# Copy and square before the exponentials: the order of ScalarE's steps in a gated recurrence over heads

## What is computed

```python
def hgrn2_mixer(h, lb, w_in, o_norm, w_o):      # 8 heads, DK = DV = 128, chunks of C = 32
    q_x, f_x, i_x, g_x = jnp.split(h @ w_in, ...)
    f = lb + (1.0 - lb) * sigmoid(f_x)
    q = heads(silu(q_x));  k = heads(1.0 - f);  log_f = heads(log(f));  v = heads(i_x)
    b = cumsum(log_f, axis=3)                    # within a chunk
    q_rel = q * exp(b - b_ref);  k_rel = k * exp(b_ref - b)
    a = where(causal, q_rel @ k_rel.T, 0.0)
    o_intra = a @ v
    q_dec = q * exp(b);  k_dec = k * exp(b_last - b);  chunk_decay = exp(b_last)
    def step(state, xs):                         # over the 16 chunks
        o_inter = qd @ state
        state = dec[..., None] * state + kd.T @ vc
        return state, o_inter
    o = o_intra + o_inter
    o = rms_norm(o, o_norm) * silu(g_x)
    return o @ w_o
```

## Time and profile before

| what | value |
|---|---|
| median of 3 runs | 1892.64 us (1892.26 to 1893.92) |
| the profiled execution | 1893.63 us, its span 1891.7 us |
| TensorE busy over the span | 1697.2 us (90%) |
| VectorE, ScalarE, POOL busy | 853.8 (45%), 716.4 (38%), 635.0 (34%) |
| mean granted clock of TensorE | 0.947 |
| the loop over heads in question | 1228.84 to 1416.94 us of the span, 188.10 us, six heads |

### The profile page before, as it was taken

The page is one execution under the profiler, slowest core; times in us unless marked ns, Lnnn a source line. Parts: engine busy times, 40 slices in busy tenths (PEclk is TensorE's granted clock), DMA queues, the critical chain, the costliest instruction groups (busy, mean ns, idle before and its releaser), DMA issues.

```text
span 1891.7 us, 29823 instructions
## 1 busy us (share of the span) xinstructions
PE 1697.2 (90%) x10588; PEld 1374.1 (73%) x10588; DVE 853.8 (45%) x1467; ACT 716.4 (38%) x1129; POOL 635.0 (34%) x385
## 2 busy tenths in 40 slices
PE   4999968768678999899999997899998899999996
PEld 4778727755455676787888887788786787888885
DVE  4634377655566444352212124667664452212124
ACT  1332333322344443461323234666663452323231
POOL 4344500002331112444444445323232453444441
PEclk8999969998888999999999998899999999999997
DMA  9423200001211112323333332222221323333331
GB/s 313 133 78 92 75 11 3 4 2 48 55 37 29 34 36 61 90 68 94 95 90 99 99 93 75 56 56 74 59 78 34 89 78 89 94 95 100 89 100 56
DMA packets 250853, 140.10 MB, mean 74 GB/s; under 512 B 10089, under 2 KB 242624, under 8 KB 250768
## 3 DMA queue, kind: packets, MB, share of 16 engines
q1 hardware_dynamic: 249072, 135.03, 24.7%
q10 hardware_dynamic: 688, 2.23, 0.3%
q0 software_dynamic: 1008, 1.66, 0.3%
HBM read 136.80 MB, written 2.10 MB: 73 GB/s over the span
## 4 chain that ended last, share of the span: by engine, by line
issue 56%; POOL 15%; PE 15%; DVE 7%; DVEq 4%; ACT 1%; POOLq 1%; DMA 1%; ACTq 0%; SPq 0%
POOL w_low L510 13%; PE bank L661 6%; PE bank L805 2%; PE bank L916 2%; DVE bank L1770 1%; DVEq L1777 1%; DVEq L2139 1%; PE bank L819 1%; DVE mix_out L1770 1%; PE bank L1021 0%; DMA w_raw<-in_mlp_w 0%; POOL param_rows L491 0%; DVE kk_norm L1770 0%; DVEq L2075 0%; PE bank L788 0%
## 5 line engine op out<-in xcount | busy, mean ns | idle before, releaser
L510 POOL TENSOR_TENSOR w_low<-w_raw,w_high 128x1024 fp32r<-128x1024 f32 (+1 forms) x232 | 513.7, 2215 | 1124.9 <-ACT w_high L1293 1124.9
L661 PE MATMUL bank<-act_high,w_high 128*128 128x512 f32 x992 | 395.7, 399 | 13.9 <-POOL w_low L510 13.8
L661 PE MATMUL bank<-act_high,w_low 128*128 128x512 f32 x992 | 388.6, 392 | 0.0
L661 PE MATMUL bank<-act_low,w_high 128*128 128x512 f32 x992 | 388.3, 391 | 0.0
L1293 ACT ACTIVATE w_high<-w_raw 128x1024 fp32r<-128x1024 f32 (+1 forms) x232 | 225.2, 971 | 299.7 <-PE bank L661 273.9
L661 PEld LDWEIGHTS bank<-act_high,w_high 128*128 128x128 f32 x992 | 187.3, 189 | 61.1 <-issue 10.2
L661 PEld LDWEIGHTS bank<-act_high,w_low 128*128 128x128 f32 x992 | 187.0, 189 | 40.6
L661 PEld LDWEIGHTS bank<-act_low,w_high 128*128 128x128 f32 x992 | 187.5, 189 | 39.5 <-issue 2.0
L661 PE MATMUL bank<-hid_high,w_high 128*128 128x512 f32 x488 | 192.0, 394 | 3.9 <-DVE mix_out L2357 3.8
L661 PE MATMUL bank<-hid_low,w_high 128*128 128x512 f32 x488 | 191.3, 392 | 0.0
L661 PE MATMUL bank<-hid_high,w_low 128*128 128x512 f32 x488 | 191.0, 391 | 0.0
(11 more groups left out here) (509 smaller groups left out, 2893.4 us busy)
## 6 DMA issues: line engine op xcount, KB each, us to landing
w_raw<-in_mlp_w SPq DMA_DIRECT2D x128, 512.0 KB, 4.0
w_raw<-in_hgrn_w_in SPq DMA_DIRECT2D x32, 512.0 KB, 4.1
w_raw<-in_w_in SPq DMA_DIRECT2D x29, 512.0 KB, 3.9
w_ada_piece<-in_w_ada SPq DMA_DIRECT2D x6, 2048.0 KB, 13.5
w_raw<-in_w_out SPq DMA_DIRECT2D x8, 512.0 KB, 3.8
w_raw<-in_mla_w_o SPq DMA_DIRECT2D x8, 512.0 KB, 3.7
w_raw<-in_hgrn_w_o SPq DMA_DIRECT2D x8, 512.0 KB, 3.7
w_raw<-in_mla_w_in SPq DMA_DIRECT2D x6, 512.0 KB, 3.9
```

Source lines behind the costliest of these rows:

```text
L510: gp.tensor_tensor(WL[:, c0 % 2, 0:kt, 0:m], WR[:, c0 % 2, 0:kt, 0:m], WH[:, c0 % 2, 0:kt, 0:m].bitcast(F32), ALU.subtract).then_inc(w_lo, 1)
L661: mm = pe.matmul(PB[s][0:m, :], w[:, s, k, 0:m], a[:, k0 + k, :], start=(k == 0 and w is WH and a is hi), stop=(k == kt - 1 and w is WL))
```

## The change

In ScalarE's `hgrn`, the block that copies and squares bank 6 for head o is put ahead of the block of five exponentials for head n. Both keep their drain and their release. The wait for `g_out` that stood before `hg_q_dec` goes, as the copy ahead of it waits for the same count. Nothing changes on another engine, and no shape or buffer changes. In the call (0, none) and in the call (none, 7) only one of the two blocks exists, and nothing moves.

```diff
--- before.py
+++ after.py
@@ -1705,22 +1705,21 @@
                         high(G0 + 3, n * 4)
                     act.wait_ge(free["g"], n * 4 + 4)
                     act.activation(QG[:, :], TG[1][:, :], ACT.Silu).then_inc(g_silu3, 1)
-                    act.wait_ge(g_diff, n + 1)
-                    act.activation(QREL[:, :], LREL[:, :], ACT.Exp)
-                    act.activation(KREL[:, :], LREL[:, :], ACT.Exp, scale=-1.0)
-                    act.activation(KDEC[:, :], TG[0][:, :], ACT.Exp)
-                    if o is not None:
-                        act.wait_ge(g_out, o + 1)
-                    act.activation(QDEC[:, :], BG[:, :], ACT.Exp)
-                    act.activation(EBL[:, :], BG[:, :].rearrange("p (c t) -> p c t", t=HC)[:, :, HC - 1], ACT.Exp)
-                    act.drain()
-                    act.sem_inc(g_exp, 1)
                 if o is not None:
                     act.wait_ge(g_out, o + 1)
                     act.activation(OG[:, :], PB[6][:, :], ACT.Copy)
                     act.activation(OSQ[:, :], PB[6][:, :], ACT.Square)
                     act.drain()
                     act.sem_inc(g_sq, 1)
+                if n is not None:
+                    act.wait_ge(g_diff, n + 1)
+                    act.activation(QREL[:, :], LREL[:, :], ACT.Exp)
+                    act.activation(KREL[:, :], LREL[:, :], ACT.Exp, scale=-1.0)
+                    act.activation(KDEC[:, :], TG[0][:, :], ACT.Exp)
+                    act.activation(QDEC[:, :], BG[:, :], ACT.Exp)
+                    act.activation(EBL[:, :], BG[:, :].rearrange("p (c t) -> p c t", t=HC)[:, :, HC - 1], ACT.Exp)
+                    act.drain()
+                    act.sem_inc(g_exp, 1)
                 if n is not None and o is not None:
                     high(G0 + 4, n * 4)
                 if o is not None:
```

## The result

The changed kernel is slower: 1901.79 us in the median of 5 runs (1900.66 to 1904.37) against 1893.56 us (1892.26 to 1893.99, 5 runs), a ratio of 1.0047 with a 95% interval of 1.0032 to 1.0061. The forecast was 1889.3 us, with a range of 1887.4 to 1891.0. The profiled execution took 1904.37 us, with a span of 1902.6.

A forecast was written before the change was run, and what follows sets the result against it. Today a ring through line 1231 takes 31.35 us per head; after the change a ring without TensorE sets 30.71. Five passages of 0.64 plus 0.12 give 3.3 us, 1892.64 - 3.3 = 1889.3 us, range 1887.4 to 1891.0.

The forecast's parts named there:

- ScalarE's part: ScalarE per head: copy at +0.53 after the Silu, Square ending +1.61, exponentials from +2.99, Sqrt at +7.93.
- the first step of TensorE's: TensorE at line 1231: follows its neighbour at 0.23 instead of 1.39, so 1.16 us earlier per head.
- Everyone who waits for `g_exp` is moved by 1.05: VectorE behind the exponentials: four products 1.05 us later, to +5.36, scaled V to +8.05; said to cost nothing.
- VectorE's cover of 1.09 us is used up to the last tenth: VectorE's wait for the Sqrt absorbs the 1.05 us delay; reciprocal starts at +8.66 instead of +8.78, gaining 0.12.
- the copy holds the exponentials up: ScalarE, slower rival: exponentials queue behind the wait for g_out; 15 us slower, 1907.6; slower rivals together 0.05.
- Ring B: Loop without TensorE, Sqrt through reciprocal, Sigmoid and scan to Sqrt: slacks 0.52 and 0.12, so 30.71 us per head.
- the likeliest case: The forecast for the loop: 0.64 us per passage, 3.3 us in all, 1889.3 us; chance 0.70.
- VectorE is late: VectorE rival: reciprocal at +8.93, behind the scaled V; ring 30.98, gain only 1.7 us, 1890.9; chance 0.12.
- The table load behind the Square: ScalarE: 0.09 + 1.29 us until the function; its slower rival added 1.28, 1896.5; slower rivals together 0.05.
- Nothing arrives: Loop rival: the Sigmoid stays where it is, the wait only moves to w_low; 1892.5 us; chance 0.03.
- TensorE takes all it can: TensorE rival: its whole 1.0 us wait per head goes, 6.0 us in all, 1886.6; chance 0.10.
- The chance of slower: Whole kernel: 0.05, split 0.03 and 0.02 over the copy's wait for outputs and a dearer table load.

The follow-up runs named there:

- e1: Changed kernel, with POOL's w_low of each head's first weight waiting for VectorE's four products; 1892.93 us against 1893.30 for the kernel before, ratio 1.0001.
- e6: e1, with POOL's w_low of each head's fourth weight also waiting for g_diff (scan and subtractions done); 1886.82 us against 1893.42, ratio 0.9962.
- e7: Kernel before, ScalarE's order untouched, with only the fourth weight's w_low waiting for g_diff; 1886.95 us, ratio 0.9968.
- e3: Kernel before, with one more 128x512 product on VectorE ahead of the four; 1894.10 us against 1893.30, ratio 1.0002.
- e4: Kernel before, with two more 128x512 products on VectorE ahead of the four; 1902.78 us, ratio 1.0050.
- e2: Changed kernel with only the Square ahead of the exponentials, the copy behind them; 1900.29 us, ratio 1.0036.

## Why the prediction was wrong, point by point

**ScalarE's part was right** to three hundredths of a microsecond up to the Sqrt, row by row, and so was the first step of TensorE's: line 1231 comes at once behind its neighbour (1265.84, then 1266.07).

**The step that failed** is the sentence on the exponentials: "Everyone who waits for `g_exp` is moved by 1.05", and then the four products are given their old durations at their new place. "VectorE's cover of 1.09 us is used up to the last tenth" was the wrong cover. The one that counted was the 0.7 us by which the last product was issued (1266.32) ahead of `w_low` (1267.01). `w_low` hangs on ScalarE's `w_high` and stays where it was (+6.67 now, +6.82 before), so 1.05 us took the last product past it, at the price of 2.2 us: 10.84 for the reciprocal is 8.66 + 2.2. Of the neighbours at the new place only ScalarE's and VectorE's own were weighed; POOL was read only for when its weight is ready.

**From 2.2 to 9.8 us.** Not every head collides: in four of the six heads of the loop the product is stretched. Then the whole ring comes later, and other things cross. The `hg_k_dec_t` and the weight come late, TensorE stands still for 1.94 and 0.80, and in the first of these heads its clock falls, as the stretch right behind shows (columns as above):

```profile
1283.40:1288.00 4.60, 3.86 (x9) 3.09 (x10) 3.25 (x9) 3.48 (x4) 3.00 (x2) 0.50 0.40 114
```

The granted clock is 0.50, its lower level of 1.2 GHz, after 1.00 up to 1280 and 0.98 in the 3.4 us from there; job G0+1 and the outputs come late by it, and the next head's copy waits 1.16 us for the outputs with the exponentials queued behind it (the last row of ScalarE above). That is the rival "the copy holds the exponentials up": it occurred in two heads (1.16 and 0.78 us), though as a consequence, and not as the cause. In these two heads `w_high` too waits for TensorE (1302.42, 0.80 us), `w_low` starts later, and the product escapes; ahead of each of them the fourth weight's `w_low` comes too late to catch the scan and stretches a subtraction behind it instead, to 2.84 and 2.03.

A head loses its time without the fall of the clock too. The head from 1328.09 has the same two waits, and a granted clock of 1.00 over its whole length (the third row of the table above):

```profile
1348.55 1.17 PE L1206 MATMUL bank<-hg_v,hg_k_dec_t 32*128 32x128 f32 x30 [1.94 <-ACT hg_k_dec_t L1695]
...
1350.52 0.49 PE L661 MATMUL bank<-act_high,w_high 128*128 128x512 f32 x1 [0.80 <-POOL w_low L510]
```

It takes 33.39 us, which is e1's 31.2 and the 2.2 of the stretched product, and the product of the head behind it is stretched again. Why the clock fell in one head and not in the other with the same waits stays open.

**The second wrong term** is the gain itself. Ring B took the scan at 2.3 us, as the rows had it, and let it move with its start. It is 1.23 us of work and a wait for POOL's `w_low`, which is released by TensorE's job G0+1. That closes a ring that I had not drawn: job G0+1, `w_high`, `w_low`, rest of the scan, Silu (10.97 after the job's start), reciprocal (8.64 later), `w_low` and with it the next job G0+1 (11.60 later): 31.21 us. It allows a gain of 0.15 per head and not of 0.64. e1, which is the prediction's own kernel without the collision, has these rows, and e6, in which the scan no longer waits, has 30.2. So the likeliest case, had only the product kept its 0.68, would have gained 1 us or less, not 3.3.

**The rivals.** "VectorE is late" had the right place, the reciprocal behind the products, and a price of 0.15 instead of 2.1. The table load behind the Square costs what the rows of the last head said, no more. "Nothing arrives" is close to what e1 shows, by another ring: the Sigmoid does come earlier (+19.48 instead of +20.14), and the scan's wait takes most of it back. The 1886.6 of "TensorE takes all it can" is about where e6 and e7 end: the slack it needed was in the scan. The chance of slower, 0.05, was on two mechanisms of which neither started it; the collision with POOL had none.

## What to carry to other kernels

Before an instruction is moved, lay it beside what *every* engine does at its new place, and ask for each pair whether one can hold the other up: VectorE with two SBUF operands and POOL reading SBUF did here. Where a VectorE instruction of one shape shows two durations in one trace (here 1.23 and 2.4 for the same scan), suspect a wait in the longer one: try the short one as its work, and look for what ends the rest, here POOL's `w_low`. And where two such instructions meet, one wait on the side that has room (POOL's weight had over 2 us) is worth more than a new order on the side that has none.

## What the runs showed of the hardware that I had not expected

Whoever of the two is issued first holds the other up for its whole instruction, and either side can be the one that pays: POOL's 2.40 us became 2.85 behind a product that ran 0.68 (e3), the product's 0.68 became 2.88 behind POOL (e4). The step lies between 0.61 and 1.22 us of delay, and in e2 a lead of 0.14 us decided it. In the profile such a wait is no idle time: the instruction shows its usual start and a longer duration. TensorE's clock was granted at its lower level behind the waits of 1.94 and 0.80 us in one head, and stayed at 1.00 behind the same waits in another; single waits of 1.00 in each head had left it at 1.00 too.
